# Reordering the steps of an eight-segment mixer recurrence: a mask ahead of an output gate, four transposes, one Gram product and two short products moved

## The chip, the cores and the metric

The kernel runs on one core of a Trainium2 chip. Its time is the device time of one execution in microseconds (us), and the figure compared is the median of several executions. The core's engines work side by side, each through its own queue in order, and meet at semaphores: TensorE (PE in the profile), VectorE (DVE), ScalarE (ACT), GpSimd (POOL) and SyncE (SP), which here issues most DMAs.

## The reference

One decoder layer on 1024 tokens of width 1024. Only the token mixers matter here; two recurrences stand in it side by side (cut):

```
def step(state, xs):                      # RWKV-7: 8 heads of 64
    r_t, w_t, k_t, v_t, kk_t, b_t = xs
    sa = einsum('bhvk,bhk->bhv', state, -kk_t)
    state = state * w_t + sa[..., None] * b_t + v_t[..., None] * k_t
    return state, einsum('bhvk,bhk->bhv', state, r_t)
...
y = (y - mu) * rsqrt(var + GN_EPS) * gn_w + gn_b     # per head
y = y + sum(r_h * k_mod * rw_r_k) * v_h
y_rw = y.reshape(bsz, seq, RW_WIDTH) * g             # g: output gate
...
# mLSTM, 4 heads of 128: C = f C + i v k^T, n = f n + i k
h = num / maximum(abs(den), exp(-m_row))             # then a norm per head
```

## The kernel before

The layer runs in stages: a feed-forward network, the input projection, the recurrences, the merge, cross-attention, a second feed-forward network. The change touches the recurrences alone, some 600 us of the span.

**Segments.** The 1024 tokens are cut into `NSEG` = 8 segments of 128. Each engine runs `iteration(i, front, back)` for i = 0 to 8. The *front* of iteration i prepares segment i, and its *back* finishes segment i - 1; iteration 0 has no back and iteration 8 no front. Each engine's order inside an iteration is the order of its code; there is no scheduler. The lists `F_PE`, `F_ACT`, `F_DVE`, `F_POOL` (front), `B_*` (back) and `M_*` (mLSTM) name every step in the order in which its engine signals it, and a wait such as `pe.wait_ge(*f_dve.at("U1", i))` means "until step U1 of this segment".

**The front on TensorE.** `turn` transposes `alpha`, `beta`, `kap` and v (in `zs`) into banks g0 and g1 (steps aT, bT, kT, vT); ScalarE copies them out (atok, btok, ktok, vtok). vT may overwrite its half of g1 only after VectorE has taken the state update dS from there, and bT its half of g0 only after VectorE has read the bonus from it (bv). Then `gram` builds A, Mu, B and Mv (8 head blocks each), and VectorE masks each out of its bank. The triangular solve takes levels n = 1 to 6 (`LEVELS` = 7). In level n TensorE makes W_n from Ur and the masked matrix am_n, ScalarE copies it (Wc) and the transposed factor (Tc), TensorE makes E_n from both, and VectorE subtracts it from Ur (U_n) and, up to `SMALL` = 4, transposes Ur (T_n). The am_n are made by GpSimd (tile AL, two slots), T0 (tile Tr) too. F, UQ, Wst, Z, gate, dC and dN end the front; dC and dN feed the mLSTM state (C, N on VectorE), gate is the product behind the output gate of the next back (gout).

**The mLSTM part** is threaded between: den in level 2, num in level 3, mean and var in levels 5 and 6; its output `myo` is stored by SP, which only then sends for the next segment's row vectors (`decays`: three broadcasts, the last into nmb). ScalarE's exponentials of these (Eb, nmb) stand ahead of its four copies atok to ktok.

**Fills.** Between the steps TensorE runs matmuls of another product, the merge gates, as filler (`gates(slot)`, source `gw`, `hq`). 24 make a unit in the one bank m1; the first matmul of a unit waits until VectorE has taken the unit before out (`empty_fill`, tile ev). The slots s7, a1, b1, b2, b3 hold 5, 6, 4, 4 and 5 matmuls, one unit together, so that slot a4 (4 matmuls, in level 4, between W4 and E4) begins the next. Iteration 3 has no fills in levels 4 to 6.

**The output of the back** (`output()` on GpSimd) scales and shifts Ys (y2, y3) and multiplies by gout (y4), after VectorE's `output_norm` (y1).

Of the kernel before, what the change touches and what calls it, by code (L numbers as in the profile page):

```python
# [149 lines left out]
F_PE = (["ss", "bonus", "aT", "vT", "bT", "kT", "A", "Mu", "am0T", "B", "W1", "E1", "Mv"]  # L150
        + [x for n in range(2, LEVELS) for x in ((f"W{n}", f"V{n - 1}", f"E{n}") if n - 1 > SMALL else (f"W{n}", f"E{n}"))]
        + ["F", f"V{LEVELS - 1}", "UQ", "Wst", "Z", "gate"])
F_ACT = (["P", "Pi", "lnn", "rinv", "atok", "vtok", "btok", "ktok", "Wc1"]
         + [x for n in range(2, LEVELS) for x in (f"Wc{n}", f"Tc{n - 1}")] + [f"Tc{LEVELS - 1}", "W1c", "Zc", "gev"])
# [2795 lines left out]
```

## Time and profile before

| | us |
|---|---|
| median of 3 runs (2834.59 to 2839.35) | 2835.09 |
| the profiled execution | 2839.34 |
| its span | 2837.5 |
| PE busy, of the span | 2742.2 (97%) |
| DVE busy | 1354.6 (48%) |
| ACT busy | 807.3 (28%) |
| POOL busy | 1523.0 (54%) |
| one inner segment (1211.90 to 1281.80) | 69.90 |
| the segment of 1281.80 to 1358.00 | 76.20 |

The profiled execution is 4.25 us above the median; 1.84 us of its time lie outside the span. Matmuls are pipelined and their ends modelled, so two groups overlap by some 0.15 us where nothing waits, and a gap in which TensorE waits is that much longer than the idle time that is printed.

### The profile page before, as it was taken

How to read it: one execution, taken by the hardware profiler on the slowest of the kernel's cores; microseconds unless marked ns; L12 is line 12 of the kernel's file. 1: busy time of each engine (PE TensorE's matmuls, PEld its weight loads, DVE VectorE, ACT ScalarE, POOL GpSimd, SP SyncE). 2: the span in 40 equal slices, each digit the busy share in tenths (PEclk: the TensorE clock that was granted, in tenths of full speed). 3: DMA queues.
4: the chain of work that ended last, by engine and by line, in shares of the span. 5: the costliest groups of instructions: out<-in, count | busy, mean ns of one | idle time of the engine just before them, and what ended most of it. 6: DMA issues, size and time to landing. Idle time of an engine off the chain costs nothing.

```text
span 2837.5 us, 35894 instructions
## 1 busy us (share of the span) xinstructions
PE 2742.2 (97%) x14234; PEld 2271.1 (80%) x14234; DVE 1354.6 (48%) x1379; ACT 807.3 (28%) x1205; POOL 1523.0 (54%) x903
## 2 busy tenths in 40 slices
PE   6999999999999989999999999999999999999998
PEld 5888888888888877777777778888987888888886
DVE  8444432014657535776777746453445444431103
ACT  5333332112001112443444323122423333331112
POOL 4988883223894623555555534330136988882221
PEclk9999999999999999998999999999999999999999
DMA  3332228361664654434243254213021333228151
GB/s 113 128 115 108 104 90 334 118 226 56 252 225 178 244 197 133 106 108 147 84 104 108 85 187 139 106 60 118 30 89 60 119 119 119 104 104 352 68 193 71
DMA packets 144520, 383.14 MB, mean 135 GB/s; under 512 B 10476, under 2 KB 61932, under 8 KB 130176
## 3 DMA queue, kind: packets, MB, share of 16 engines
q1 hardware_dynamic: 110144, 299.92, 30.1%
q10 hardware_dynamic: 34240, 81.30, 7.8%
q8 instruction: 98, 1.61, 0.2%
q14 instruction: 38, 0.31, 0.0%
HBM read 272.57 MB, written 108.58 MB: 134 GB/s over the span
## 4 chain that ended last, share of the span: by engine, by line
PE 43%; issue 9%; POOL 7%; DVE 2%; DMA 1%; ACT 0%; POOLq 0%; SPq 0%; DVEq 0%; ACTq 0%
PE G L1068 7%; PE G L1070 7%; PE G L1069 7%; PE G L993 5%; PE G L994 5%; PE G L995 5%; POOL AL L879 2%; PE G L1238 2%; PE G L1537 1%; PE G L1519 1%; PE G L1275 1%; POOL Tr L873 1%; DMA nmb<-rows_d 0%; POOL rho L862 0%; PE G L1504 0%
## 5 line engine op out<-in xcount | busy, mean ns | idle before, releaser
L950 POOL TENSOR_TENSOR whi<-raw,zero 128x1024 fp32r<-128x1024 f32 x67 | 140.0, 2089 | 431.6 <-PE G L995 343.4
L1068 PE MATMUL G<-hhi,v_hi 128*128 128x512 f32 x800 | 312.0, 390 | 0.0
L1070 PE MATMUL G<-hhi,v_lo 128*128 128x512 f32 x800 | 311.2, 389 | 0.0
L1069 PE MATMUL G<-hlo,v_hi 128*128 128x512 f32 x800 | 311.2, 389 | 0.0
L934 POOL TENSOR_TENSOR v_lo<-sum_temp,v_hi 128x512 fp32r<-128x512 f32 x88 | 115.3, 1311 | 357.0 <-ACT v_hi L1750 357.0
L993 PE MATMUL G<-hhi,whi 128*128 128x512 f32 x688 | 271.1, 394 | 22.1 <-POOL wlo L953 20.1
L994 PE MATMUL G<-hlo,whi 128*128 128x512 f32 x688 | 269.8, 392 | 0.0
L995 PE MATMUL G<-hhi,wlo 128*128 128x512 f32 x688 | 269.6, 392 | 0.0
L1238 PE MATMUL G<-hq,gw 128*128 128x512 f32 x768 | 220.2, 419 | 12.6 <-DVE ev L2548 10.1
L1068 PE MATMUL G<-t_hi,whi 128*128 128x512 f32 x480 | 186.8, 389 | 0.0
L1070 PE MATMUL G<-t_hi,wlo 128*128 128x512 f32 x480 | 186.7, 389 | 0.0
L1069 PE MATMUL G<-t_lo,whi 128*128 128x512 f32 x480 | 186.7, 389 | 0.0
L953 POOL TENSOR_TENSOR wlo<-raw,whi 128x1024 fp32r<-128x1024 f32 x67 | 178.1, 2658 | 5.2
L1238 PEld LDWEIGHTS G<-hq,gw 128*128 128x128 f32 x768 | 136.7, 191 | 50.2 <-issue 26.0
L1068 PEld LDWEIGHTS G<-hhi,v_hi 128*128 128x128 f32 x800 | 150.2, 188 | 31.6 <-issue 0.5
L1069 PEld LDWEIGHTS G<-hlo,v_hi 128*128 128x128 f32 x800 | 150.2, 188 | 31.6 <-issue 0.5
L1070 PEld LDWEIGHTS G<-hhi,v_lo 128*128 128x128 f32 x800 | 150.1, 188 | 31.2
L993 PEld LDWEIGHTS G<-hhi,whi 128*128 128x128 f32 x688 | 130.5, 190 | 51.2 <-POOL wlo L953 20.9
L930 POOL TENSOR_TENSOR wlo<-sum_temp,whi 128x512 fp32r<-128x512 f32 x120 | 164.9, 1395 | 3.6 <-ACT whi L1734 3.6
L1750 ACT ACTIVATE v_hi<-sum_temp 128x512 fp32r<-128x512 f32 x88 | 55.8, 634 | 373.1 <-PE G L1070 317.0
L994 PEld LDWEIGHTS G<-hlo,whi 128*128 128x128 f32 x688 | 130.5, 190 | 27.5 <-issue 0.2
L995 PEld LDWEIGHTS G<-hhi,wlo 128*128 128x128 f32 x688 | 130.4, 190 | 27.4
(426 smaller groups left out, 6280.8 us busy)
## 6 DMA issues: line engine op xcount, KB each, us to landing
a_d<-act_new SPq DMA_DIRECT2D x20, 2048.0 KB, 6.3
atile<-a_d SPq DMA_DIRECT2D x36, 1024.0 KB, 10.0
gw<-gw_d SPq DMA_DIRECT2D x32, 1024.0 KB, 5.4
raw<-in_wg SPq DMA_DIRECT2D x44, 512.0 KB, 4.0
sum_temp<-in_wd ACTq DMA_DIRECT2D x82, 256.0 KB, 3.6
xT<-in_wu SPq DMA_DIRECT2D x40, 512.0 KB, 4.3
...
```

Source lines behind the costliest of these rows:

```text
L879: tt(AL[:, n % 2], Am[:], copies(C_LEV + n * P), ALU.mult).then_inc(*F.sig(f"am{n}"))
L930: tt(slot(False, n), src, slot(True, n).bitcast(F32), ALU.subtract).then_inc(f_lo.sem, 1)
L934: tt(v_lo[:, k, :], wd_raw[b % WD_RAWS][:], v_hi[:, k, :].bitcast(F32), ALU.subtract).then_inc(f_lo.sem, 1)
L950: nc.gpsimd.tensor_tensor(whi[:, k, 0:w], raw[:, k, 0:w], zero[:].to_broadcast([P, w]), ALU.add).then_inc(hi_made, 1)
L953: nc.gpsimd.tensor_tensor(wlo[:, k, 0:w], raw[:, k, 0:w], whi[:, k, 0:w].bitcast(F32), ALU.subtract).then_inc(split_made, 1)
L993: nc.tensor.matmul(dst, wh, hi, start=start, stop=False)
L994: nc.tensor.matmul(dst, wh, lo, start=False, stop=False)
L995: return nc.tensor.matmul(dst, wl, hi, start=False, stop=stop)
L1068: nc.tensor.matmul(dst, wh, hi, start=start, stop=False, skip_group_check=True)
L1069: nc.tensor.matmul(dst, wh, lo, start=False, stop=False, skip_group_check=True)
L1070: return nc.tensor.matmul(dst, wl, hi, start=False, stop=stop, skip_group_check=True)
L1238: last = nc.tensor.matmul(G[3][:, 1, :], gw[:, k, way == 2, t * P:(t + 1) * P], hq[:, t + (way == 1) * KD, :], start=at == 0, stop=at == 3 ...
```

## The change

Five moves, no instruction added or removed:

1. GpSimd: am1 is made ahead of T0; `output()` is split, with y2 and y3 still after am3, and y4 after am4.
2. TensorE's transposes run alpha, kap, beta, v, and ScalarE copies them in that order. VectorE computes bv ahead of dS and S.
3. The Gram product Mv and its mask move from level 1 to level 4 (`MV_AT`).
4. dN (4 products, the mLSTM normalizer) moves from the end of the front to ahead of UQ.
5. The product gate moves from behind Z to ahead of Wst.

```diff
-F_POOL = ["rk", "rkb", "kap", "rho", "T0"] + [f"am{n}" for n in range(1, LEVELS)] + ["IU"]
+F_POOL = ["rk", "rkb", "kap", "rho", "am1", "T0"] + [f"am{n}" for n in range(2, LEVELS)] + ["IU"]
...
-            tt(Tr[:], copies(C_ID), AL[:, 0].bitcast(F32), ALU.subtract).then_inc(*F.sig("T0"))
             for n in range(1, LEVELS):
                 if n == 2:
+                    tt(Tr[:], copies(C_ID), AL[:, 0].bitcast(F32), ALU.subtract).then_inc(*F.sig("T0"))
                     pool.wait_ge(*F.at("T0", i))
...
                 if n == 3 and back:
-                    output()
+                    output_scale()
+                if n == 4 and back:
+                    output_gate()
...
                 turn(g0[:, 0, :], alpha).then_inc(*F.sig("aT"))
-                pe.wait_ge(*b_dve.at("dS", j))
+                pe.wait_ge(*f_pool.at("kap", i))
                 pe.wait_ge(*f_dve.at("Q", i - 1))
-                turn(g1[:, 1, :], zs[:, 8:12, :]).then_inc(*F.sig("vT"))
+                turn(g1[:, 0, :], kap).then_inc(*F.sig("kT"))
                 pe.wait_ge(*f_dve.at("bv", i))
                 turn(g0[:, 1, :], beta).then_inc(*F.sig("bT"))
-                pe.wait_ge(*f_pool.at("kap", i))
-                turn(g1[:, 0, :], kap).then_inc(*F.sig("kT"))
+                pe.wait_ge(*b_dve.at("dS", j))
+                turn(g1[:, 1, :], zs[:, 8:12, :]).then_inc(*F.sig("vT"))
...
-                pe.wait_ge(*f_act.at("ktok", i))
+                pe.wait_ge(*f_act.at("vtok", i))
                 gram(alpha, beta, g1).then_inc(*F.sig("A"))
...
                 if n > 1:
                     gates(f"a{n}")
+                if n == MV_AT:
+                    pe.wait_ge(*b_dve.at("ve", j))
+                    gram(kap, rho, g2).then_inc(*F.sig("Mv"))
                 pe.wait_ge(*f_act.at(f"Wc{n}" if n == 1 else f"Tc{n - 1}", i))
                 eight(g0, Tr, Wr).then_inc(*F.sig(f"E{n}"))
-                if n == 1:
-                    pe.wait_ge(*b_dve.at("ve", j))
-                    gram(kap, rho, g2).then_inc(*F.sig("Mv"))
                 gates(f"b{n}")
```

The hunks on dN and gate in TensorE's code, on bv and on Mv's mask in VectorE's, and on the order of ScalarE's copies move the same lines to the places named above.

TensorE, levels 1 and 4 of an inner segment, before (first row: E1; fourth: W2; after the dots W4, its fills, E4 and its fills; `rho,kap` is Mv):

```order
L1275 MATMUL G0<-Wr_124,Tr_123 128x128 x8
L1269 MATMUL G2<-rho_109,kap_108 128x128 x8
L1238 MATMUL G3<-hq_164,gw_165 128x512 x4
L1275 MATMUL G1<-Ur_122,AL_127 128x128 x8
...
L1275 MATMUL G1<-Ur_122,AL_127 128x128 x8
L1238 MATMUL G3<-hq_164,gw_165 128x512 x4
L1275 MATMUL G0<-Wr_124,Tr_123 128x128 x8
L1238 MATMUL G3<-hq_164,gw_165 128x512 x5
```

The same two places of the changed kernel:

```order
L1284 MATMUL G0<-Wr_124,Tr_123 128x128 x8
L1247 MATMUL G3<-hq_164,gw_165 128x512 x4
L1284 MATMUL G1<-Ur_122,AL_127 128x128 x8
...
L1284 MATMUL G1<-Ur_122,AL_127 128x128 x8
L1247 MATMUL G3<-hq_164,gw_165 128x512 x4
L1278 MATMUL G2<-rho_109,kap_108 128x128 x8
L1284 MATMUL G0<-Wr_124,Tr_123 128x128 x8
L1247 MATMUL G3<-hq_164,gw_165 128x512 x5
```

Mv has left the place between E1 and W2 and stands between the fills of slot a4 and E4.

GpSimd, from kw to the state's decay (CN), before:

```order
L871 TENSOR_TENSOR kw_150<-mktok_151,Db_147 128x512
L873 TENSOR_TENSOR Tr_123<-cst_49,AL_127 128x1024
L879 TENSOR_TENSOR AL_127<-Am_117,cst_49 128x1024 x3
L845 TENSOR_TENSOR Ys_136<-Ys_136,vec_50 128x512
L847 TENSOR_TENSOR Ys_136<-Ys_136,bvb_140 128x512
L850 TENSOR_TENSOR yo_141<-Ys_136,gout_110 128x512
L879 TENSOR_TENSOR AL_127<-Am_117,cst_49 128x1024
L884 TENSOR_TENSOR CN_156<-CN_156,Eb_145 128x1024
```

And in the changed kernel:

```order
L878 TENSOR_TENSOR kw_150<-mktok_151,Db_147 128x512
L886 TENSOR_TENSOR AL_127<-Am_117,cst_49 128x1024
L882 TENSOR_TENSOR Tr_123<-cst_49,AL_127 128x1024
L886 TENSOR_TENSOR AL_127<-Am_117,cst_49 128x1024 x2
L848 TENSOR_TENSOR Ys_136<-Ys_136,vec_50 128x512
L850 TENSOR_TENSOR Ys_136<-Ys_136,bvb_140 128x512
L886 TENSOR_TENSOR AL_127<-Am_117,cst_49 128x1024
L856 TENSOR_TENSOR yo_141<-Ys_136,gout_110 128x512
```

One mask now stands ahead of Tr, and the fourth mask ahead of yo.

TensorE, the end of a front, before (fills of slot F, UQ, then Wst, Z, gate, dC, dN):

```order
L1238 MATMUL G3<-hq_164,gw_165 128x512 x2
L1275 MATMUL G0<-Qr_125,Tr_123 128x128 x8
...
L1434 MATMUL G2<-Uf_121,atok_112 64x128 x8
L1438 MATMUL G0<-vtok_115,Bm_118 128x64 x8
L1442 MATMUL G2<-gsig_95,loraw_93 128x128 x4
L1446 MATMUL G0<-mvtok_152,kw_150 128x128 x4
L1450 MATMUL G3<-cst_49,kw_150 128x128 x4
```

And in the changed kernel:

```order
L1247 MATMUL G3<-hq_164,gw_165 128x512 x2
L1438 MATMUL G3<-cst_49,kw_150 128x128 x4
L1284 MATMUL G0<-Qr_125,Tr_123 128x128 x8
...
L1446 MATMUL G2<-gsig_95,loraw_93 128x128 x4
L1451 MATMUL G2<-Uf_121,atok_112 64x128 x8
L1455 MATMUL G0<-vtok_115,Bm_118 128x64 x8
L1459 MATMUL G0<-mvtok_152,kw_150 128x128 x4
```

dN stands ahead of UQ, gate ahead of Wst, and dC is last.

## Rows read from the trace of the kernel before

**Rows 1.** Windows view: stretch, length, busy PE, PEld, DVE, ACT, POOL, clock, DMA.

```profile
1211.90:1281.80 69.90, 66.09 (x536) 54.24 (x535) 51.25 (x64) 29.79 (x55) 38.98 (x25) 1.00 0.37 104
1281.80:1358.00 76.20, 68.90 (x510) 57.25 (x509) 50.23 (x63) 29.22 (x53) 38.90 (x25) 0.87 0.41 138
```

**Rows 2.** Timeline of TensorE, levels 1 and 4, segment 2: start, duration, idle before.

```profile
1237.95 1.08 PE L1275 MATMUL G<-Ur,AL 128*128 128x128 f32 x8 [0.52 <-POOL AL L879]
...
1240.28 1.03 PE L1275 MATMUL G<-Wr,Tr 128*128 128x128 f32 x8
1241.24 1.16 PE L1269 MATMUL G<-rho,kap 64*128 64x128 f32 x16
...
1254.25 1.08 PE L1275 MATMUL G<-Ur,AL 128*128 128x128 f32 x8 [0.95 <-DVE Uf L2670]
...
1256.96 1.11 PE L1275 MATMUL G<-Wr,Tr 128*128 128x128 f32 x8 [0.66 <-ACT Tr L1989]
```

**Rows 3.** Timeline of GpSimd, same segment.

```profile
1233.07 2.39 POOL L873 TENSOR_TENSOR Tr<-cst,AL 128x1024 fp32r<-128x1024 f32 x1 [1.57 <-DVE AL L2640]
1235.43 7.51 POOL L879 TENSOR_TENSOR AL<-Am,cst 128x1024 fp32r<-128x1024 f32 x3
1247.68 1.04 POOL L845 TENSOR_TENSOR Ys<-Ys,vec 128x512 f32<-128x512 f32 x1 [4.74 <-DVE Ys L2572]
1248.80 1.27 POOL L847 TENSOR_TENSOR Ys<-Ys,bvb 128x512 f32<-128x512 f32 x1
1250.24 1.53 POOL L850 TENSOR_TENSOR yo<-Ys,gout 128x512 f32<-128x512 f32 x1 [0.16 <-POOL Ys L847]
1251.72 2.38 POOL L879 TENSOR_TENSOR AL<-Am,cst 128x1024 fp32r<-128x1024 f32 x1
```

**Rows 4.** Timeline of VectorE, same segment.

```profile
1238.27 1.32 DVE L2563 COPY_PREDICATED Bm<-cst,G 128x1024 f32<-128x1024 uint32 x1
...
1243.24 0.38 DVE L2674 TENSOR_TENSOR S0s<-St,Pi 128x256 f32<-128x256 f32 x1
...
1249.40 1.22 DVE L2657 TENSOR_TENSOR aden<-aden,nmb 128x512 f32<-128x512 f32 x1
...
1254.16 0.65 DVE L2548 TENSOR_TENSOR ev<-G,hq 128x512 f32<-128x512 f32 x1
```

**Rows 5.** Timeline of VectorE in iteration 0, the step dmax.

```profile
1110.99 0.65 DVE L2657 TENSOR_TENSOR aden<-aden,nmb 128x512 f32<-128x512 f32 x1
```

**Rows 6.** Timeline of TensorE in iteration 0, slot a4.

```profile
1116.41 1.17 PE L1238 MATMUL G<-hq,gw 128*128 128x512 f32 x4 [0.68 <-DVE ev L2548]
```

**Rows 7.** Timeline of TensorE, transpose of beta and Gram product A, segment 2.

```profile
1226.69 0.65 PE L1263 MATMUL G<-cst,beta 128*128 128x128 f32 x4 [0.41 <-DVE bv L2624]
...
1228.57 1.16 PE L1269 MATMUL G<-beta,alpha 64*128 64x128 f32 x16
```

**Rows 8.** Timeline of ScalarE: Eb in segments 2, 5, 7, segment 7's last copy.

```profile
1224.91 0.63 ACT L1956 ACTIVATE Eb<-Eb 128x512 f32<-128x512 f32 x1 [2.77 <-DMA nmb<-rows_d]
...
1440.36 0.63 ACT L1956 ACTIVATE Eb<-Eb 128x512 f32<-128x512 f32 x1 [2.31 <-DMA nmb<-rows_d]
...
1581.34 0.63 ACT L1956 ACTIVATE Eb<-Eb 128x512 f32<-128x512 f32 x1 [3.50 <-DMA nmb<-rows_d]
...
1583.83 0.61 ACT L1963 ACTIVATE ktok<-G 128x512 f32<-128x512 f32 x1
```

**Rows 9.** Timeline of TensorE, ends of fronts: UQ, Wst, dN; last, segment 7's Wst.

```profile
1272.45 1.11 PE L1275 MATMUL G<-Qr,Tr 128*128 128x128 f32 x8 [0.43 <-ACT Tr L2000]
...
1274.88 1.09 PE L1434 MATMUL G<-Uf,atok 128*64 128x128 f32 x16 [0.22 <-DVE Uf L2689]
...
1279.58 1.06 PE L1450 MATMUL G<-cst,kw 128*128 128x128 f32 x8
...
1630.49 1.56 PE L1434 MATMUL G<-Uf,atok 128*64 128x128 f32 x16 [1.31 <-DVE Uf L2689]
```

**Rows 10.** Timeline of TensorE in iteration 3, E4.

```profile
1326.80 1.65 PE L1275 MATMUL G<-Wr,Tr 128*128 128x128 f32 x8 [1.63 <-ACT Tr L1989]
```

More of the change, by code:

```diff
@@ L149 @@
 L_PE, L_ACT, L_POOL = ["lora"], ["th", "ad", "tw", "ta", "gt"], ["kkr", "sq"]
[L150 to L153, printed above, removed]
+MV_AT = SMALL
+F_PE = (["ss", "bonus", "aT", "kT", "bT", "vT", "A", "Mu", "am0T", "B", "W1", "E1"]
+        + [x for n in range(2, LEVELS) for x in [f"W{n}"] + [f"V{n - 1}"] * (n - 1 > SMALL) + ["Mv"] * (n == MV_AT)
+           + [f"E{n}"]]
+        + ["F", f"V{LEVELS - 1}", "UQ", "gate", "Wst", "Z"])
+F_ACT = (["P", "Pi", "lnn", "rinv", "atok", "ktok", "btok", "vtok", "Wc1"]
          + [x for n in range(2, LEVELS) for x in (f"Wc{n}", f"Tc{n - 1}")] + [f"Tc{LEVELS - 1}", "W1c", "Zc", "gev"])
 F_DVE = (["dec", "scan", "hend", "cc", "gs", "av", "gu", "kmod", "ssc", "n1", "n2", "rin", "kk", "kka",
-          "alpha", "beta", "bv", "pend", "A", "am0", "Mu", "U0", "B", "U1", "T1", "S0s", "Mv"]
-         + [x for n in range(2, LEVELS) for x in ((f"U{n}", f"T{n}") if n <= SMALL else (f"U{n}",))] + ["Q", "Uf"])
-F_POOL = ["rk", "rkb", "kap", "rho", "T0"] + [f"am{n}" for n in range(1, LEVELS)] + ["IU"]
+          "alpha", "beta", "bv", "pend", "A", "am0", "Mu", "U0", "B", "U1", "T1", "S0s"]
+         + [x for n in range(2, LEVELS) for x in [f"U{n}"] + [f"T{n}"] * (n <= SMALL) + ["Mv"] * (n == MV_AT)]
+         + ["Q", "Uf"])
+F_POOL = ["rk", "rkb", "kap", "rho", "am1", "T0"] + [f"am{n}" for n in range(2, LEVELS)] + ["IU"]
 B_PE = ["U", "Y", "dS", "mean", "var"]
@@ L162 @@
 B_POOL = ["bvb", "ysq", "y2", "y3", "y4"]
-M_PE = ["kT", "vT", "S", "den", "num", "mean", "var", "dC", "dN"]
+M_PE = ["kT", "vT", "S", "den", "num", "mean", "var", "dN", "dC"]
 M_ACT = ["gtok", "ktok", "E", "nm", "vtok", "D", "aden", "lnv", "rsv"]
@@ L841, in iteration, with output_scale @@
             j = i - 1
-            def output():
+            def output_scale():
                 pool.wait_ge(*b_dve.at("y1", j))
@@ L880, in iteration @@
                 if n == 3 and back:
-                    output()
+                    output_scale()
+                if n == 4 and back:
+                    output_gate()
                 if n == 4:
@@ L1426, in iteration @@
             gates("F")
+            pe.wait_ge(*m_dve.at("ve", i))
+            for h in range(MH):
+                last = nc.tensor.matmul(m0[:, h * SEG:(h + 1) * SEG], kw[:, h, :], con(C_ONES), start=True, stop=True)
+            last.then_inc(*M.sig("dN"))
             pe.wait_ge(*f_act.at(f"Tc{LEVELS - 1}", i))
@@ L1431, in iteration @@
                 ahead(i + 1)
+            for r in range(RC):
+                last = nc.tensor.matmul(g2[:, 0, r * P:(r + 1) * P], loraw[:, 1, r * P:(r + 1) * P], gsig[:],
+                                        start=True, stop=True)
+            last.then_inc(*F.sig("gate"))
             pe.wait_ge(*f_dve.at("Uf", i))
@@ L1440, in iteration @@
             last.then_inc(*F.sig("Z"))
-            for r in range(RC):
-                last = nc.tensor.matmul(g2[:, 0, r * P:(r + 1) * P], loraw[:, 1, r * P:(r + 1) * P], gsig[:],
-                                        start=True, stop=True)
-            last.then_inc(*F.sig("gate"))
             for h in range(MH):
@@ L1447, in iteration @@
             last.then_inc(*M.sig("dC"))
-            pe.wait_ge(*m_dve.at("ve", i))
-            for h in range(MH):
-                last = nc.tensor.matmul(m0[:, h * SEG:(h + 1) * SEG], kw[:, h, :], con(C_ONES), start=True, stop=True)
-            last.then_inc(*M.sig("dN"))
         def merge():
@@ L2615, in iteration @@
                         empty_fill(f)
+            if front:
+                dve.wait_ge(*f_pe.at("bonus", i))
+                dve.wait_ge(*b_pool.at("bvb", j))
+                tt(bv[:], three(g0[:, 1, :]), zs[:, 8:12, :], ALU.mult).then_inc(*F.sig("bv"))
             if back:
```

16 lines of the change are left out of this document (8 added, 8 removed).

## The prediction

> **What bounds the kernel now.** I read the windows view first. In an inner segment of 69.90 us TensorE is busy for 66.09, VectorE for 51.25, GpSimd for 38.98 and ScalarE for 29.79 [rows 1]. So TensorE sets the pace, and a reordering that adds no instruction can take at most its waits: 3.8 us of idle time, a little more with the 0.15 us of overlap that each wait also undoes. Next I read TensorE's timeline of one inner segment for its gaps, and behind each gap the timeline of the engine that it waits for. The gaps: 0.52 before W1 [rows 2], 0.95 before W4 and 0.66 before E4 [rows 2], some 0.7 in the transposes, of which 0.41 before beta's [rows 7], 0.43 before UQ and 0.22 before Wst [rows 9]. These repeat in segments 1 to 7. The trace names VectorE's transpose for the wait before W4, but W4 needs am4 and U3, and am4 ends at 1251.72 + 2.38 = 1254.10, just ahead of W4 at 1254.25 [rows 2, 3]: GpSimd's y2, y3 and y4, from 1247.68 to 1251.77, hold it.
>
> I follow one segment round from UQ to the next UQ and write how much earlier each station comes.
>
> **The tail (moves 4 and 5).** TensorE is free for UQ at about 1271.80 and starts it at 1272.45 [rows 9]. dN costs 0.81 (from 1279.58 to the next fill at 1280.39) [rows 9] and fills that wait, so UQ comes 0.2 late. gate's eight matmuls cost 1.11 - 0.15 = 0.96, as UQ's eight do [rows 9], and cover the whole wait of Wst for Uf (0.22 + 0.15). TensorE thus reaches the next segment some 1.0 us earlier: 0.65 + 0.38. Little of it is kept. VectorE's chain to alpha starts when dC ends, which is now only 0.2 earlier, since dC is last; and the DMA chain (UQ, Uf, the mLSTM norm, myo, its store, three broadcasts, nmb) starts 0.2 later. TensorE will wait 0.6 to 0.7 before alpha's transpose, where it hardly waits now.
>
> **The transposes (move 2).** Now dS, S and bv stand in a row on VectorE between alpha and beta's transpose at 1226.69 [rows 7]. Behind alpha the new order needs bv (0.69), then dS; A could start 0.8 earlier relative to alpha, 1.0 in all. But A also waits for ScalarE's four copies, which stand behind Eb, and Eb waits for nmb's DMA. Eb to the last copy's end takes 1583.83 + 0.61 - 1581.34 = 3.10 when nothing holds it [rows 8]. With the DMA 0.2 later, A comes at Eb + 3.35: in segment 2 at 1228.26 against 1228.57 [rows 7, 8], 0.3 earlier; in segment 5, whose Eb began at 1440.36, 0.8 earlier; in segment 7 0.2 later [rows 8]. Over the seven segments, with each one's Eb, I get 0.27 on average. The bounds are 0.2 lost and 1.0 gained.
>
> **W1 (move 1, first half).** am1 would end one mask's time (2.36) earlier [rows 3], so W1 waits for nothing but TensorE: 0.52 + 0.15 = 0.67. Its result is used by E1, which also needs VectorE's Bm, ending at 1239.59 while E1 starts at 1240.28 [rows 2, 4]. That leaves 0.63. T0 would end at 1237.8, long before E1.
>
> **Levels 1 to 3 (move 3).** Between E1 and W2 Mv costs 1241.24 to 1242.3, 1.0 [rows 2], and W2 needs U1 at the end of the fills only. VectorE loses Mv's mask (1.3, a Bm's time) ahead of output_norm and U2, so that U2, y1 and all behind come 1.2 earlier. But S0s, at 1243.24 now [rows 4], would fall into the time of am3, which ends at 1235.43 + 7.51 = 1242.94 [rows 3] and does not move with E1. Two rows show what such a meeting costs: dmax took 1.22 us where it began with 0.67 of y3 to go (1249.40 against 1248.80 + 1.27 = 1250.07) [rows 3, 4], and 0.65 with GpSimd idle [rows 5]. So S0s ends 0.33 later than it would alone. W4 would need am4, which now follows y3 instead of y4 (1.5 us saved): it ends about when U3 and the fills do. W4 comes 2.35 - 0.33 = 2.0 earlier relative to E1.
>
> The Trainium skill says the same of that meeting (SBUF — State Buffer, § Who interferes with whom): with two inputs in SBUF a VectorE instruction is fully blocked until GpSimd's ends. Without that rule the segment would gain 0.33 us more, 2.3 over seven.
>
> **Level 4: a new wait.** Slot a4 begins a unit of fills, and its first matmul waits for VectorE's ev. Now ev (1254.16 to 1254.81) is over before the slot at 1255.17 [rows 4], because W4 is late. VectorE's ev follows U3 and T3, which come only 1.19 - 0.33 earlier, while W4 comes 2.0 earlier: the fills would wait 0.9 us. Iteration 0, where no output holds am4, shows just this wait, 0.68 before slot a4 [rows 6]. Queued behind it on TensorE are Mv and E4. ev ends at E1 + 13.7, four fills (0.9) and Mv (1.0) bring E4 to E1 + 15.6, where it is at E1 + 16.68 now [rows 2]. From E1 to E4 the segment gains 1.05, not 2.1. E4's own wait for ScalarE (0.66) is covered by Mv. W5 and later levels keep their distances; am5, behind y4 and CN, ends 0.3 to 0.6 ahead of W5.
>
> **Sum.** An inner segment: 0.27 + 0.63 + 1.05 = 1.95, six times: 11.7. Iteration 3 has no fill in slot a4 and gains 0.27 + 0.63 + 1.9 = 2.8. Iteration 0 is held by Bm and by ev already and loses only Mv's place: 0.75. Segment 7's end waits 0.4 before UQ and 1.31 + 0.15 before Wst [rows 9]; dN and gate fill most: 1.5. Together 16.8 us. Against the profiled execution's own 2839.3 that is 2822.6; that execution lies 4.25 us above the median, and from the median the sum is **2818.3 us**, 0.6% faster.
>
> **The clock.** In iteration 3 TensorE's mean granted clock is 0.87 of 2.4 GHz, in the segment before it 1.00 [rows 1]; it fell to 1.2 GHz behind the wait of 1.63 before E4 [rows 10] and cost some 6 us. Mv would stand in that wait and gate in the 1.31 of segment 7. The gain by this is 0 to 9 us; I take 0, since only the level after it would tell, and keep it in the range.
>
> **The rivals.**
> (a) *More*: the DMA lands earlier by chance of its queue, or S0s escapes am3, or iteration 3 keeps its full clock. Each is worth 7 x 0.7 = 5, 7 x 0.33 = 2.3, and up to 6 us; two of them give 2810. For it: TensorE's gap there is filled. Against: VectorE's and ScalarE's chains in iteration 3 stay sparse.
> (b) *Less*: the end of the front is a circle through the DMA, and a segment gets back only W4's 1.0 and a part of W1's: the mask or a copy stands in the way of E1. 7 x 1.1 = 8 gives 2827. For it: Bm ends only 0.69 before E1 now. Against: B's product hangs on Mu's mask, which keeps its distance to A.
> (c) *The changed order does nothing*: TensorE's waits were already covered by something else in the circle, as a DMA-bound front would do: 2835. Against: A's start is not DMA-bound in most segments [rows 8].
> (d) *Slower*: the new wait of 0.9 before a4 together with 0.65 before alpha lowers the clock in each segment. Iteration 3's fall cost 6 us in one segment; half of that, 3 us in each of seven, outweighs 16.8 and gives 2839. It decides from 2.4 us a segment. Against: a wait of 0.95 at that very place in six segments, at a clock of 1.00 [rows 1, 2].
>
> **How the numbers follow.** Forecast (2814 to 2824) 0.50, (a) 0.22, (b) 0.20, (c) 0.05, (d) 0.03. A measurement of this kernel tells about 0.2% from no change, here 5.7 us: faster means below 2829.4. So faster 0.92, same 0.05, slower 0.03. The range of 8 in 10 reaches into (a) and (b): 2809 to 2827.
>
> **What would show it.** Right: inner segments of about 68 us; no GpSimd wait before W1 or W4; ev named before slot a4; no wait before E4, UQ or Wst; a wait of 0.6 before alpha's transpose; ScalarE's Eb still behind nmb's DMA. Wrong: A starting 0.8 earlier after alpha in all segments would put the DMA term too high; no ev wait before a4 would put level 4 at 2 us; a clock below 1.00 in inner segments would be (d).

## The result, and the profile after

| | before | after |
|---|---|---|
| median, us | 2837.22 (2834.59 to 2839.77) | 2819.95 (2816.52 to 2821.87) |
| ratio | | 0.9941 [0.9928, 0.9954] |
| the profiled execution | 2839.34 | 2816.52 |
| its span | 2837.5 | 2814.7 |

The changed kernel is 0.6% faster: 17.3 us by the medians. That of before is of four executions now, 2.1 above the 2835.09 from which the forecast starts. The two profiled executions lie 22.8 apart, and that is the number to be careful with: the execution of before lies 2.1 above its median, that of after 3.4 below. Line numbers of after are some 9 higher. Both have the same instructions; that TensorE's busy time falls from 2742.2 to 2730.4 us fits its clock, as the next view shows. The page's busy line of after:

```profile
PE 2730.4 (97%) x14234; PEld 2263.7 (80%) x14234; DVE 1364.8 (48%) x1379; ACT 805.1 (29%) x1205; POOL 1513.6 (54%) x903
```

Windows view of after, an inner segment and the one that holds iteration 3; columns as in [rows 1]:

```profile
1209.50:1277.40 67.90, 65.70 (x537) 54.36 (x535) 51.58 (x64) 29.61 (x54) 38.97 (x25) 1.00 0.36 108
1277.40:1347.70 70.30, 64.81 (x512) 53.67 (x511) 50.89 (x63) 29.74 (x54) 39.48 (x26) 0.93 0.47 148
```

TensorE's idle time in the inner segment was 69.90 - 66.09 = 3.81 [rows 1] and is 67.90 - 65.70 = 2.20. In the other the granted clock was 0.87 [rows 1] and is 0.93: at 1.2 GHz for about 2 x 0.13 x 76.2 = 20 us before and 2 x 0.07 x 70.3 = 10 after.

TensorE's timeline of after, segment 2 (start, duration, idle before): the transpose of alpha, A, then levels 1 and 4, and last dN and UQ.

```profile
1223.32 0.66 PE L1272 MATMUL G<-cst,alpha 128*128 128x128 f32 x4 [0.73 <-DVE alpha L2619]
...
1226.49 1.16 PE L1278 MATMUL G<-beta,alpha 64*128 64x128 f32 x16
...
1235.15 1.11 PE L1284 MATMUL G<-Ur,AL 128*128 128x128 f32 x8
...
1237.53 1.07 PE L1284 MATMUL G<-Wr,Tr 128*128 128x128 f32 x8
...
1249.40 1.00 PE L1284 MATMUL G<-Ur,AL 128*128 128x128 f32 x8
1251.20 1.15 PE L1247 MATMUL G<-hq,gw 128*128 128x512 f32 x4 [0.79 <-DVE ev L2557]
1252.28 1.16 PE L1278 MATMUL G<-rho,kap 64*128 64x128 f32 x16
1253.37 1.11 PE L1284 MATMUL G<-Wr,Tr 128*128 128x128 f32 x8
...
1268.31 1.05 PE L1438 MATMUL G<-cst,kw 128*128 128x128 f32 x8
1269.11 1.09 PE L1284 MATMUL G<-Qr,Tr 128*128 128x128 f32 x8
```

W1 waits for nothing (it waited 0.52 for GpSimd's mask), W4 for nothing (0.95), E4 for nothing (0.66) [rows 2]. Two waits are new: 0.73 before alpha's transpose, and 0.79 for VectorE's ev ahead of the four fills behind W4. Mv and E4 stand in the queue behind those fills.

GpSimd's and VectorE's timelines beside it:

```profile
1230.89 2.39 POOL L886 TENSOR_TENSOR AL<-Am,cst 128x1024 fp32r<-128x1024 f32 x1 [1.56 <-DVE AL L2651]
1233.23 2.39 POOL L882 TENSOR_TENSOR Tr<-cst,AL 128x1024 fp32r<-128x1024 f32 x1
1235.79 5.00 POOL L886 TENSOR_TENSOR AL<-Am,cst 128x1024 fp32r<-128x1024 f32 x2 [0.17 <-POOL Tr L882]
...
1246.28 2.82 POOL L886 TENSOR_TENSOR AL<-Am,cst 128x1024 fp32r<-128x1024 f32 x1
1249.06 1.28 POOL L856 TENSOR_TENSOR yo<-Ys,gout 128x512 f32<-128x512 f32 x1
```

```profile
1240.54 0.53 DVE L2687 TENSOR_TENSOR S0s<-St,Pi 128x256 f32<-128x256 f32 x1
...
1250.40 0.65 DVE L2557 TENSOR_TENSOR ev<-G,hq 128x512 f32<-128x512 f32 x1
```

am1 (1230.89) now precedes T0 (Tr); am4 ends at 1246.28 + 2.82 = 1249.10, just ahead of W4, and y4 follows it. S0s meets am3, which ends at 1235.79 + 5.00 = 1240.79, and takes 0.53 instead of 0.38 [rows 4]: 0.15 more, where 0.25 of am3 was left.

The end of segment 7 (TensorE: UQ, gate, Wst; the last row is the back's first product):

```profile
1610.53 1.09 PE L1284 MATMUL G<-Qr,Tr 128*128 128x128 f32 x8
1611.45 1.10 PE L1446 MATMUL G<-gsig,loraw 128*128 128x128 f32 x8
1612.93 1.09 PE L1451 MATMUL G<-Uf,atok 128*64 128x128 f32 x16 [0.37 <-DVE Uf L2701]
...
1617.13 2.00 PE L1308 MATMUL G<-Zm,Uf 128*128 128x64 f32 x16 [0.24 <-ACT gout L2020]
```

Wst waited 1.31 there, and took 1.56 where it takes 1.09 in other segments [rows 9]. The windows view of before and of after for this end:

```profile
1626.00:1639.30 13.30, 11.60 (x78) 10.72 (x77) 6.33 (x8) 2.57 (x5) 4.00 (x4) 0.74 0.39 138
```

```profile
1603.00:1617.00 14.00, 13.53 (x111) 11.99 (x109) 7.01 (x9) 4.58 (x8) 3.16 (x3) 1.00 0.28 95
```

The clock is 0.74 before and 1.00 after: the fall came behind the wait of 1.31 and is absent behind that of 0.37.

### The profile page after: what moved, and what is told of

The parts are those of the page before. It is cut to its first block, busy times and chain, and to the rows that moved or that the text cites. A ratio compares the mean times of both kernels' runs of the same rounds, so it can differ in the third digit from the quotient of the medians.

```text
span 2814.7 us, 35894 instructions
## 1 busy us (share of the span) xinstructions
PE 2730.4 (97%) x14234; PEld 2263.7 (80%) x14234; DVE 1364.8 (48%) x1379; ACT 805.1 (29%) x1205; POOL 1513.6 (54%) x903
## 4 chain that ended last, share of the span: by engine, by line
PE 78%; issue 10%; POOL 7%; DVE 3%; DMA 1%; ACT 1%; SPq 1%; ACTq 0%; POOLq 0%; DVEq 0%
PE G L1077 15%; PE G L1078 15%; PE G L1079 15%; PE G L1002 8%; PE G L1004 8%; PE G L1003 8%; PE G L1247 2%; POOL AL L886 2%; PE G L1546 1%; PE G L1528 1%; PE G L1284 1%; DVE nt_b L2196 1%; POOL Tr L882 1%; DMA nmb<-rows_d 0%; POOL rho L868 0%
## 5 line engine op out<-in xcount | busy, mean ns | idle before, releaser
L1247 PE MATMUL G<-hq,gw 128*128 128x512 f32 x768 | 219.6, 418 | 17.4 <-DVE ev L2557 14.7
```

The lines of the kernel that those rows point to most:

```text
L1247: last = nc.tensor.matmul(G[3][:, 1, :], gw[:, k, way == 2, t * P:(t + 1) * P], hq[:, t + (way == 1) * KD, :], start=at == 0, stop=at == 3 ...
```

## The experiments

A *segment* below runs from the start of the back's first product (`Zm,Uf`) to that of the next segment. An inner one is 1, 2, 4, 5 or 6 (the middle value of the five stands in the table); "3" is the one with iteration 3, "7" the last. These three come from the profiled execution alone; the medians and ratios from all executions, each ratio against before on the same chip. The medians come from several chips, on which that of before is 2836.5 to 2839.8, so kernels are compared by ratio. The profiled execution is not always a typical one: mv_first's was the slowest of its five, 7.8 above the median.

| kernel | inner, us | 3, us | 7, us | median, us | ratio to before |
|---|---|---|---|---|---|
| before | 69.87 | 76.58 | 70.99 | 2837.2 | |
| after | 67.88 | 70.31 | 65.62 | 2819.9 | 0.9941 [0.9928, 0.9954] |
| only_masks | 68.91 | 75.00 | 70.04 | 2832.1 | 0.9982 [0.9972, 0.9991] |
| only_turns | 69.06 | 75.81 | 72.08 | 2835.9 | 0.9993 [0.9982, 1.0005] |
| only_mv | 69.06 | 72.98 | 70.23 | 2830.6 | 0.9975 [0.9966, 0.9985] |
| only_tail | 70.08 | 76.59 | 67.68 | 2835.8 | 0.9995 [0.9985, 1.0004] |
| no_tail | 67.78 | 72.69 | 76.10 | 2830.8 | 0.9962 [0.9948, 0.9976] |
| no_mv | 68.37 | 72.26 | 68.30 | 2825.1 | 0.9952 [0.9938, 0.9965] |
| mv_first | 67.18 | 74.17 | 68.74 | 2816.1 | 0.9921 [0.9907, 0.9934] |
| dc_first | 68.27 | 68.38 | 69.47 | 2830.0 | 0.9965 [0.9953, 0.9977] |
| decays_first | 67.86 | 70.22 | 70.19 | 2818.2 | 0.9922 [0.9905, 0.9938] |
| eb_late | 68.32 | 71.13 | 65.84 | 2819.5 | 0.9931 [0.9914, 0.9947] |
| eb_mv | 67.56 | 70.63 | 65.09 | 2813.5 | 0.9904 [0.9887, 0.9920] |
| eb_last_mv_dc | 66.41 | 70.57 | 64.87 | 2810.2 | 0.9900 [0.9884, 0.9916] |

### One move alone, on the kernel before

**only_masks**: move 1 alone.

```diff
-F_POOL = ["rk", "rkb", "kap", "rho", "T0"] + [f"am{n}" for n in range(1, LEVELS)] + ["IU"]
+F_POOL = ["rk", "rkb", "kap", "rho", "am1", "T0"] + [f"am{n}" for n in range(2, LEVELS)] + ["IU"]
...
                 if n == 3 and back:
-                    output()
+                    output_scale()
+                if n == 4 and back:
+                    output_gate()
```

> The kernel before with move 1 alone (am1 ahead of T0, y4 after am4). Theory (a circle of stations in which slot a4's fills wait for ev): W1 0.6 us earlier; am4 ends 1.5 us earlier, so W4 starts 1.1 us earlier, but the fills of slot a4 then wait about 0.8 us for ev, since VectorE still carries Mv's mask in level 1. Inner segment 68.4 to 68.6 us instead of 69.88, some 10 us faster in all. Rival (each wait is worth its own length, no new one): 0.67 + 1.1 = 1.8 us a segment, 68.1, 13 us in all.

Measured: -0.96 an inner segment, from 69.87 to 68.91, where 68.4 to 68.6 was expected. The waits before W1 and W4 are gone, and the wait for ev is there at once (TensorE, slot a4):

```profile
1253.20 1.16 PE L1244 MATMUL G<-hq,gw 128*128 128x512 f32 x4 [0.80 <-DVE ev L2554]
```

So a part of the gain goes into a wait already with move 1 alone. A second wait is new, and the expectation missed it: TensorE waits 0.31 before W5 for am5, since am4 has moved ahead of y4 and am5 has not. GpSimd's order was the cause of both old waits; that the trace named VectorE before W4 [rows 2] was the last event, not the cause.

**only_turns**: move 2 alone.

```diff
 turn(g0[:, 0, :], alpha)
-turn(g1[:, 1, :], zs[:, 8:12, :])   # behind dS
+turn(g1[:, 0, :], kap)
 turn(g0[:, 1, :], beta)             # behind bv
-turn(g1[:, 0, :], kap)
+turn(g1[:, 1, :], zs[:, 8:12, :])   # behind dS
```

> The kernel before with move 2 alone (transposes alpha, kap, beta, v; bv ahead of dS). Theory (A waits for whichever comes last, the four copies behind nmb's DMA or the transposes behind alpha): inner segments 0.3 to 0.8 us shorter, differently from segment to segment with the landing of the DMA, 69.3 on average, 3 to 4 us in all. Rival (only the transposes behind alpha count): 0.8 us in every segment, 69.1, 5.6 us in all. Rival (only the DMA counts): nothing.

Measured: some 0.8 less in four of five inner segments, but 71.78 in segment 2 and 72.08 in segment 7; no difference that shows in the median. Segment 2 on TensorE:

```profile
1228.64 1.16 PE L1269 MATMUL G<-beta,alpha 64*128 64x128 f32 x16 [0.88 <-ACT vtok L1963]
...
1241.56 1.08 PE L1275 MATMUL G<-Wr,Tr 128*128 128x128 f32 x8 [1.55 <-DVE Bm L2563]
```

A waits for the last copy, behind the DMA and Eb. The second wait has its cause one step up, on VectorE:

```profile
1237.43 2.81 DVE L2653 SCALAR_TENSOR_TENSOR qe<-zm,Eb 128x512 f32<-128x512 f32 x1 [0.34 <-PE G L1269]
1240.17 1.29 DVE L2563 COPY_PREDICATED Bm<-cst,G 128x1024 f32<-128x1024 uint32 x1
```

and GpSimd at that time:

```profile
1234.98 7.49 POOL L879 TENSOR_TENSOR AL<-Am,cst 128x1024 fp32r<-128x1024 f32 x3
```

The second of the three masks, seen by itself:

```profile
1237.32 2.38 POOL L879 TENSOR_TENSOR AL<-Am,cst 128x1024 fp32r<-128x1024 f32 x1
```

qe starts 0.11 behind this mask's start and ends 0.54 behind its end. It took 2.81 instead of 0.68 to 0.91. The prediction priced such a meeting for S0s alone.

**only_mv**: move 3 alone.

```diff
-                if n == 1:
+                if n == MV_AT:
                     pe.wait_ge(*b_dve.at("ve", j))
                     gram(kap, rho, g2).then_inc(*F.sig("Mv"))
```

> The kernel before with move 3 alone (Mv and its mask in level 4). Theory: E1 to W4 1.2 us shorter, because VectorE's output_norm starts a mask earlier and GpSimd's y2 to y4 and am4 with it; no wait for ev before slot a4, since W4 still waits for am4; E4 1.0 us earlier relative to E1; inner segment 68.9 us, 8 us in all, and up to 6 more if iteration 3's clock stays up. Rival (Mv only fills E4's own wait of 0.66, all else unchanged): 0.8 us a segment, 69.1. Rival (a product of 1 us before E4 costs what it saves in level 1): 69.9.

Measured: 69.06 (68.9 was expected), -0.81 an inner segment. It has the largest gain of a single move in the median, though its interval overlaps that of only_masks.

**only_tail**: moves 4 and 5 alone.

```diff
-        + ["F", f"V{LEVELS - 1}", "UQ", "Wst", "Z", "gate"])
+        + ["F", f"V{LEVELS - 1}", "UQ", "gate", "Wst", "Z"])
-M_PE = [..., "mean", "var", "dC", "dN"]
+M_PE = [..., "mean", "var", "dN", "dC"]
```

> The kernel before with moves 4 and 5 alone (dN ahead of UQ, gate ahead of Wst). Theory: TensorE reaches the next segment 1.0 us earlier and waits 0.7 to 0.9 us for alpha there, since VectorE's chain starts only 0.2 us earlier; inner segment 69.7 us; segment 7's end 1.5 us shorter at its old clock and 3 us more if the fall to 1.2 GHz there does not come; 3 to 6 us in all. Rival (TensorE is the bound, so both waits are gained): 1.0 us a segment, 68.9, 9 us in all.

Measured: +0.2 an inner segment, to 70.08, where a small gain (69.7) was expected, and alpha's transpose waits 0.73. In segment 7 it is -3.3, to 67.68: gate fills the wait before Wst down to 0.37, and the clock doesn't fall there. That this is move 5's doing, and no chance of one execution, shows across the kernels. All five with gate behind Z (before, only_masks, only_turns, only_mv, no_tail) wait 1.31 before Wst, and the clock of the 7 us from 1 us behind Wst's start is 0.50 to 0.56. In the seven that wait 0.37 it is 1.00.

In inner segments the four single gains are 0.96, 0.81, 0.81 and -0.21: 2.37, where all moves together give 1.99. Some is paid twice; moves 1 and 3 both bring W4 forward against ev. By the medians of the same chip the four moves gain 4.8, 1.0, 6.3 and 1.1 us, where 10, 3 to 4, 8 and 3 to 6 were expected. By the ratios the singles sum to 1.8 + 0.7 + 2.5 + 0.5 = 5.5 thousandths, all together 5.9 ± 1.3: no difference can be told there.

### The change without one move

**no_tail** (moves 4 and 5 undone):

```diff
-        + ["F", f"V{LEVELS - 1}", "UQ", "gate", "Wst", "Z"])
+        + ["F", f"V{LEVELS - 1}", "UQ", "Wst", "Z", "gate"])
```

> The changed kernel with moves 4 and 5 undone (dN last, gate behind Z). Theory after the four single moves (the tail moves cost an inner segment 0.2 us, since UQ comes 0.2 later and alpha does not come earlier; they pay only in segment 7, where nothing waits behind them): inner segments 67.7 us instead of 67.9, six of them 1.2 us less; the end of segment 7 longer by 1.5 us, and by some 4 more if its clock falls to 1.2 GHz again as in the kernel before; 2820 to 2824 in all, equal or slower than the change by up to 4. Rival (the tail's two waits are worth their length once the others are gone): inner segments 68.9, 7 us slower than the change.

**no_mv** (move 3 undone):

```diff
-                if n == MV_AT:
+                if n == 1:
                     gram(kap, rho, g2).then_inc(*F.sig("Mv"))
```

> The changed kernel with move 3 undone (Mv and its mask in level 1). Theory: VectorE's output_norm and U2 are a mask later again, ev too, and the fills of slot a4 wait for it; E4 no longer waits behind Mv, but W2 does. From the single moves' inner segments (69.88 before; 68.94, 69.08 and 70.08 with moves 1, 2 and 4+5): 68.3 us against 67.88 with the change, 3 us slower in all. Iteration 3: TensorE lacks Mv in its gap before E4, and its clock falls for some 20 us as before, 3 us more. Rival (Mv's place is worth nothing beside am4's): 67.9.

Without the tail's moves the middle inner segment is as short as after (67.78, as expected), so these give nothing there. The median missed: 2830.8 for 2820 to 2824. Segment 7 is 76.10 instead of 65.62. On VectorE there:

```profile
1582.52 2.86 DVE L2662 SCALAR_TENSOR_TENSOR qe<-zm,Eb 128x512 f32<-128x512 f32 x1 [0.36 <-PE G L1278]
```

E1 waited 1.76 behind it, and from 1600 to 1633 the mean clock was 0.84. Not all of the 10.5 us is the tail's: qe meets a mask in segment 7 of no_mv, mv_first, dc_first and decays_first too, which keep the tail's moves and take 68.3 to 70.2 there. The whole change without these moves is 0.9962, with them 0.9941: the intervals overlap, the direction is that of segment 7. Without Mv's move a segment is 68.37, as expected: 0.5 longer, where Mv alone was worth 0.8. Not all of the 0.5 is Mv's, since A waits 0.32 to 0.72 for vtok, behind the DMA, in four of the five segments.

### One move more

**mv_first**: Mv ahead of the fills of slot a4.

```diff
-                if n > 1:
-                    gates(f"a{n}")
                 if n == MV_AT:
                     pe.wait_ge(*b_dve.at("ve", j))
                     gram(kap, rho, g2).then_inc(*F.sig("Mv"))
+                if n > 1:
+                    gates(f"a{n}")
```

> The changed kernel with Mv ahead of slot a4's fills in level 4 instead of behind them. Theory (the fills' wait of 0.79 us for ev is real and Mv can cover it): the wait before the fills goes, E4 starts 1.0 us earlier (then just behind ScalarE's Tc3), W5 0.9 us earlier, at the end of am5; inner segments 67.0 us, iteration 3 unchanged (no fills there), 2813 to 2814 in all. Rival (W5 is held by am5 or U4 and everything is only moved one step on): 67.8.

TensorE in level 4 (W4, Mv, fills, E4):

```profile
1249.66 1.00 PE L1284 MATMUL G<-Ur,AL 128*128 128x128 f32 x8
1250.60 1.16 PE L1278 MATMUL G<-rho,kap 64*128 64x128 f32 x16
1251.69 1.18 PE L1247 MATMUL G<-hq,gw 128*128 128x512 f32 x4
1252.71 1.00 PE L1284 MATMUL G<-Wr,Tr 128*128 128x128 f32 x8
```

The wait for ev is gone, and W4 to E4 takes 3.05 instead of 3.97. Of the inner segments three are 67.0 to 67.2, as expected, and two 67.9 to 68.0: in those A waits 0.91 and 1.05 for vtok, behind the DMA. The ratio is 0.9921; its interval overlaps that of the change. Its iteration 3 has the order of the changed kernel's, and yet takes 74.17 at a clock of 0.86, where that took 70.31 at 0.93. So a difference of 4 us in the column "3" can be one of executions.

**dc_first**: on the changed kernel, dC ahead of Wst, so that VectorE's chain to alpha starts earlier.

```diff
             pe.wait_ge(*f_dve.at("Uf", i))
+            for h in range(MH):
+                last = nc.tensor.matmul(g0[:, 1, h * SEG:(h + 1) * SEG], kw[:, h, :], mvtok[:, h, :], ...)
+            last.then_inc(*M.sig("dC"))
             for n, e, r, rows in heads:      # Wst, Z
```

> The changed kernel with dC ahead of Wst and Z, so that VectorE's C, N and the chain to alpha can start 1.5 us earlier. Theory (two chains end together at A: alpha's on VectorE and nmb's DMA with the six ScalarE steps behind it, 3.14 us from Eb to A): the wait of 0.73 before alpha's transpose goes, but A comes only as early as Eb + 3.14, which is 0 to 0.4 us; inner segments 67.7, 1 us in all. Rival (alpha's chain alone bounds the front): 0.7 us or more in each segment, 67.1, 5 us in all.

Alpha is no longer waited for, yet the segments get longer, 67.7 to 68.5; 67.7 was expected, and the rival's 67.1 is further off. The ratio, 0.9965, is worse than the change's by 2.4 thousandths, some 7 us, and the intervals hardly overlap. TensorE and ScalarE, segment 2:

```profile
1231.50 1.16 PE L1278 MATMUL G<-beta,alpha 64*128 64x128 f32 x16 [1.54 <-ACT vtok L1972]
```

```profile
1228.35 0.63 ACT L1965 ACTIVATE Eb<-Eb 128x512 f32<-128x512 f32 x1 [4.14 <-DMA nmb<-rows_d]
```

A follows Eb by 3.15 in every segment: behind the wait for alpha stood a second one, for the broadcasts. These also landed later here. From the store's issue to Eb it takes 14.0 to 15.0 us, where it took 13.3 to 14.1 in the changed kernel; from UQ to the store it takes 8.4 in both. What delayed the landing is not shown. In segment 7, behind Z, the back's first product waits 1.19 for gout, and the clock falls there too. This raised the question which of the two bounds the changed kernel.

### Alpha or the DMA?

**decays_first**: SyncE issues the broadcasts ahead of the store of myo.

```diff
             sp.wait_ge(*m_pool.at("y3", i))
-            sp.dma_start(segment(y_d[0:RC], i), myo[:]).then_inc(ym_out, 16)
             if more:
                 decays(i + 1)
+            sp.dma_start(segment(y_d[0:RC], i), myo[:]).then_inc(ym_out, 16)
```

> The changed kernel, but SyncE issues the three broadcasts of the next segment's rows ahead of the store of myo, which they don't need. Theory (DMA bounds A): the landing comes earlier by one issue and the store's share of the queue, 0.1 to 0.6 us; idle time before Eb falls from 3.26 to about 2.9 and A follows by as much until alpha's transpose bounds it (0.4): segments 67.5, median 1 to 3 us below the changed kernel. Rival (SyncE's wait for the myo of this segment, not the issue order, sets the landing, since the broadcasts are of the same length whatever stands ahead): 13.3 to 14.4 us from issue to landing as before, segments 67.9.

ScalarE's idle time before Eb falls from 3.26 to 2.71 in segment 2, more than expected, but the segments stay at 67.86, where 67.5 was expected. TensorE:

```profile
1222.87 0.65 PE L1273 MATMUL G<-cst,alpha 128*128 128x128 f32 x4 [0.73 <-DVE alpha L2620]
```

```profile
1222.34 0.63 ACT L1966 ACTIVATE Eb<-Eb 128x512 f32<-128x512 f32 x1 [2.71 <-DMA nmb<-rows_d]
```

A stands at 1225.96, 3.09 behind the transpose; after, it was 3.17. So the DMA cost the changed kernel 0.08 in segment 2. Its own trace says the same of the others: A follows alpha's transpose by 3.28 in segment 1, and by 3.08 or 3.09, as here, in 4, 5 and 6. The theory that the DMA bounds A in the inner segments fell; alpha does, as long as the broadcasts land as early as in that execution. In segment 7, where A waits 0.35 for vtok, it is the DMA. There decays_first takes 70.19, since qe meets a mask (2.89). (The two kernels' medians differ by 1.7 us, within their spread.)

**eb_late**: on ScalarE, the exponentials of Eb and nmb behind the four copies.

```diff
-                act.wait_ge(bc_in, i * 48 + 48)
-                activation(flat(Eb[:]), flat(Eb[:]), ACT.Exp).then_inc(*M.sig("E"))
-                activation(flat(nmb[:]), ...)
                 for name, dst, src in (("a", atok, ...), ...):
                     ...
+                act.wait_ge(bc_in, i * 48 + 48)
+                activation(flat(Eb[:]), flat(Eb[:]), ACT.Exp).then_inc(*M.sig("E"))
+                activation(flat(nmb[:]), ...)
```

> The changed kernel with one further move on ScalarE: the exponentials of Eb and nmb, which wait for the three broadcasts, go behind the four copies atok to vtok instead of ahead of them. Theory (A's start is bound by the DMA through ScalarE's order: in all runs with the new order of transposes vtok ends 3.1 us behind the start of Eb): A no longer follows Eb; it follows the last transpose. alpha ends at 1223.3, vT cannot come before dS is taken (1224.8), a transpose and a copy give A at 1226.05 instead of 1226.49. Segments of 67.4 to 67.5 instead of 67.9, and all alike; median 2.5 to 3 us below the changed kernel, about 2817. VectorE's step arg still waits for the DMA, but A's mask starts 4.9 us behind its landing, so that doesn't bind. Rival (the DMA bounds nothing, A is bound by alpha and dS): segments stay 67.9. Rival 2 (the copies met by the exponentials move the wait: Db, behind Eb, comes late and holds Pb on VectorE): segments longer than 68.

A is again 3.09 behind alpha's transpose, but the segments are 68.32, 0.44 longer. Db, behind Eb now, ends later, and with it GpSimd's kw:

```profile
1228.49 1.05 POOL L878 TENSOR_TENSOR kw<-mktok,Db 128x512 f32<-128x512 f32 x1 [0.81 <-ACT Db L1978]
```

```profile
1228.94 1.68 DVE L2651 TENSOR_TENSOR AL<-Am,cst 128x1024 fp32r<-128x1024 f32 x1
```

am0 on VectorE starts inside kw (until 1229.54) and takes 1.68 instead of 1.23. That 0.45 is the loss of 0.44. The second rival had the right place (Db late) and the wrong mechanism: nothing waited for Pb; the fills behind ev, which follows am0 on VectorE, wait 0.58.

**eb_mv**: eb_late and mv_first together.

> As eb_late, and in level 4 Mv stands ahead of the fills of slot a4, which took the wait for VectorE's ev away. Theory: the two gains add: segments of 66.5 to 66.7 all alike, where Mv ahead alone gave 67.0 to 67.2 in some and 67.9 in others as the DMA landed; span about 7 x 0.8 = 5.6 us below that of Mv ahead alone without its slow segments, median 2811 to 2813. Rival: once A is early the circle is held elsewhere (alpha, U1 or VectorE), and segments stay at 67.0 to 67.2, median 2815.

Segments of 67.56, all alike but the shorter fourth (66.97): mv_first's 67.1 and the same 0.45. The expectation of 66.5 to 66.7 missed. Against eb_late this is the cleanest measure of Mv's place ahead of the fills, since no DMA stands before A in either: each inner segment is 0.75 to 0.77 shorter, and the medians, from one chip, lie 6.0 apart (2809.9 to 2814.4 against 2817.2 to 2821.0, no overlap). Its median of 2813.5 lies just above the forecast's 2811 to 2813: segment 7, with 65.09, made up for the others.

**eb_last_mv_dc**: mv_first and dc_first, and the exponentials behind Db as well, so that neither the copies nor Db nor kw waits for the DMA.

```diff
-                act.wait_ge(bc_in, i * 48 + 48)
-                activation(flat(Eb[:]), flat(Eb[:]), ACT.Exp).then_inc(*M.sig("E"))
-                activation(flat(nmb[:]), ...)
                 ...                                    # copies, mvtok, Db
+                act.wait_ge(bc_in, i * 48 + 48)
+                activation(flat(Eb[:]), flat(Eb[:]), ACT.Exp).then_inc(*M.sig("E"))
+                activation(flat(nmb[:]), ...)
...
+            dve.wait_ge(*m_act.at("E", i))             # ahead of qe
...
+                    pool.wait_ge(*m_act.at("E", i))    # ahead of CN
```

> Three moves on top of the changed kernel: Mv ahead of the fills of slot a4, dC ahead of Wst (so that VectorE's chain to alpha starts about 1 us earlier), and the exponentials of Eb and nmb, which wait for the broadcasts, behind the four copies, the mLSTM's v copy and Db on ScalarE, so that neither A nor VectorE's Pb stands behind the DMA any longer. With dC early alone, alpha was no longer waited for, but A waited 1.0 to 2.1 us for vtok behind Eb, in every segment. Theory (the circle is alpha or the DMA in front of A, whichever is later, and Pb behind Db where Eb stands ahead of Db): with both gone A follows alpha's transpose by 3.1 us, without a wait for vtok, and a segment is 0.7 us (the wait before alpha) shorter than with Mv early alone: 66.2 to 66.5, against 67.57 with Eb behind the copies but ahead of Db; median 2805 to 2808. Rival (TensorE's circle is held behind A by VectorE's masks or by dS whatever comes first): segments of 67.0 or more, median 2812 or more.

Windows view, an inner segment and the one with iteration 3:

```profile
1208.00:1274.40 66.40, 65.74 (x537) 54.24 (x535) 52.41 (x64) 29.85 (x54) 39.95 (x25) 1.00 0.39 110
1274.40:1345.00 70.60, 66.43 (x513) 54.75 (x511) 52.38 (x63) 29.84 (x54) 40.51 (x25) 0.90 0.47 148
```

Segments of 66.4 as expected, with TensorE idle for 66.40 - 65.74 = 0.66, against 3.81 before. A neither waits for a copy nor alpha's transpose for alpha; A follows that by 3.09. The median missed by 2 us (2810.2 for 2805 to 2808): iteration 3 stayed at 70.6 with a clock of 0.90. At 0.9900 [0.9884, 0.9916] this kernel is faster than both; against the changed kernel that is some 10 us. Its time against eb_mv's 0.9904 can't be told apart by the ratios, though the segments are 1.15 us shorter: 0.73 for alpha's wait and 0.45 for am0, which takes 1.23 again, less 0.03.

## Why the prediction was right, point by point

The forecast was 2818.3 in 2809 to 2827; the median is 2819.95. The gain is 17.3 for 16.8 predicted, with 13 to 20 as the interval of the ratio. Inner segments of "about 68" are 67.88, -1.99 for -1.95. Its terms, from the timelines of segment 2:

| | predicted | measured |
|---|---|---|
| tail, DMA, transposes: UQ to UQ by way of A | 0.27 | 0.73 to A, less 0.24 by which UQ is late: 0.49 |
| A to E1 | 0.63 | 11.71 to 11.04: 0.67 |
| E1 to W4 | 2.0 | 13.97 to 11.87: 2.10 |
| the new wait for ev | 0.9 | 0.79 |
| E1 to E4 | 1.05 | 16.68 to 15.84: 0.84 |

- **The tail.** Right: a wait of 0.73 before alpha's transpose for 0.6 to 0.7, and UQ 0.24 late for 0.2. It gives nothing in an inner segment (only_tail, no_tail).
- **The transposes and the DMA.** The term that was mis-sized most: 0.49 for 0.27. It was sized by the DMA, 0.2 later than before, with A 3.15 behind Eb. Measured, A stands 3.14 or 3.15 behind Eb in segments 1, 2 and 7, and 3.22 to 3.53 in 3 to 6, where alpha's chain bounds it. And the DMA landed earlier and not later: from the store's issue to Eb it took 13.59 on average, 14.04 before. That is rival (a)'s first case, and an execution's luck as far as is known. What held the gain at 0.49 was alpha: A stands 3.09 behind its transpose for 3.88 before, the 0.8 that was predicted from that side, but alpha itself comes hardly earlier behind UQ (22.12 to 22.09 in segment 2), where the prediction had its chain start 0.2 earlier. In segment 2 the two bounds lie within 0.1, over the seven within 0.4.
- **W1 and levels 1 to 3.** Right in place and size. S0s lost 0.15 to am3 and not 0.33: it began 0.25 before am3's end.
- **Level 4.** The four fills take 1.08 from start to start and Mv 1.09, where I took 0.9 and 1.0: 0.27 too little, so that E4 gained 0.84 and not 1.05. mv_first shows the wait's price from the other side, 0.9 from W4 to E4. I weighed the wait and didn't ask whether Mv and the fills need stand in that order.
- **Iteration 3 and segment 7.** Mis-sized in the profile pair: 2.8 and 1.95 + 1.5 = 3.45 were predicted; the profiles say 76.58 - 70.31 = 6.27 and 70.99 - 65.62 = 5.37. What exceeds it, 5.4 us, goes with the clock, which I had put at 0 in the forecast, with 0 to 9 in the range: 10 us less at 1.2 GHz in iteration 3 and 2 x 0.26 x 13.3 = 7 less at segment 7's end are worth half of that, 8.5, at most. TensorE in iteration 3 (Mv, E4, W5; the clock falls here):

```profile
1318.20 1.16 PE L1278 MATMUL G<-rho,kap 64*128 64x128 f32 x16
1319.90 1.11 PE L1284 MATMUL G<-Wr,Tr 128*128 128x128 f32 x8 [0.54 <-ACT Tr L1998]
1322.54 1.08 PE L1284 MATMUL G<-Ur,AL 128*128 128x128 f32 x8 [1.53 <-POOL AL L886]
1323.46 1.39 PE L1418 MATMUL G<-hm,cst 128*128 128x512 f32 x2
1325.25 1.97 PE L1284 MATMUL G<-Wr,Tr 128*128 128x128 f32 x8 [0.41 <-ACT Tr L1998]
```

  The wait before E4 shrank from 1.63 [rows 10] to 0.54, but one of 1.53 stands before W5, and E5 takes 1.97 instead of 1.11. With one wait filled, the fall came behind the next, and lasted 10 us instead of 20. For segment 7 the cause is shown (only_tail). For iteration 3 it is not: mv_first, with the same order there, lost 20 us of full clock as before, and no_mv, with the wait of 1.63 still there, has 0.91.
- **Iteration 0.** Right: 0.77 for 0.75, from alpha's transpose to the back's first product (57.95 to 57.18). Its start lay 0.35 later in the profiled execution of after, in stages that the change leaves alone.
- **Why the median still fits.** Before's executions spread with the mean granted clock that each shows: those at 0.989 to 0.990 took 2833.4 to 2837.8, those at 0.986 2839.3 to 2842.2 (31 executions on one chip). The four of after are all at 0.990, 2816.5 to 2821.9. So some of the clock gain may belong in the median too. How much, these runs can't say: the terms without it come to what was predicted or a little more, and the interval of the gain is 7 us wide. That the gain came within 0.5 us of its forecast is closer than it can be measured, and so partly luck.
- **The rivals.** (a) has its part in iteration 3's clock and in the earlier landings, both in the profiled execution. (d) did not come: the clock is 1.00 in inner segments with both new waits in place. (b) is seen in only_turns, by a meeting that nobody had priced. It was there to be read in the kernel before: in its iteration 0 qe takes 2.68, and E1 waits 1.56 for Bm.

What decides over qe is who starts first. Two segments of mv_first, 5 and 7, show it, each with qe and the mask beside it:

```profile
1444.89 0.69 DVE L2662 SCALAR_TENSOR_TENSOR qe<-zm,Eb 128x512 f32<-128x512 f32 x1 [0.36 <-PE G L1278]
1444.95 2.89 POOL L886 TENSOR_TENSOR AL<-Am,cst 128x1024 fp32r<-128x1024 f32 x1 [0.17 <-PE G L1278]
...
1580.25 2.90 DVE L2662 SCALAR_TENSOR_TENSOR qe<-zm,Eb 128x512 f32<-128x512 f32 x1 [0.35 <-PE G L1278]
1580.20 2.39 POOL L886 TENSOR_TENSOR AL<-Am,cst 128x1024 fp32r<-128x1024 f32 x1
```

Where qe starts 0.06 ahead of the mask, it takes 0.69 and the mask 2.89; where it starts 0.05 behind, the mask takes 2.39 and qe 2.90. The price for VectorE is what is left of GpSimd's instruction, less 0.10 to 0.15: for S0s 0.15 with 0.25 left, for qe in the changed kernel (from 1235.27, 0.90 long) 0.21 with 0.35 left of Tr, for qe in only_turns 2.12 with 2.27 left, for am0 in eb_late 0.45 with 0.60 left. The Trainium skill (SBUF — State Buffer, § Who interferes with whom) says that a VectorE instruction with two SBUF inputs contends with a GpSimd instruction that reads SBUF, over ports that are an exclusive lock. The runs agree: the later one waits for the rest of the first, less that tenth or so.
